# Waits in the order of their producers, implied waits left out, one semaphore per queue for a channel tile's shift transfers

## The chip, the cores and the metric

The kernel runs on the 8 cores of one Trainium2 chip, the same program on each with its own data, and the cores exchange nothing. The time is that of the slowest core in device microseconds, the median of 3 runs. Engines are named as in the profile: PE (TensorE matmul), PEld (its weight load), DVE (VectorE), ACT (ScalarE), POOL (GpSimd), SP (SyncE). A q behind an engine's name is its sequencer, which waits and issues while the engine itself is idle.

## The reference

One inference step of an encoder trunk of four layers, D_MODEL 1024, D_INNER 2048, for 4 x 4096 prompt tokens and 8 x 32 sample tokens. Each layer is an RMSNorm with a shift and scale, an input projection, a mixer, a SiLU gate, an output projection and a residual add. The part that the change touches most is the mixer of layer 2:

```python
            a, ag, z = jnp.split(jnp.einsum('bsd,de->bse', h, w_in_c), 3, axis=-1)
            glu = a * jax.nn.sigmoid(ag)
            ext, conv_c_new = with_history(glu, hist_c, CCONV_W - 1)
            y = causal_depthwise_conv(ext, w_conv_c) + b_conv_c
            y = jax.nn.silu(layer_norm(y, ln_c_g, ln_c_b))
            out = jnp.einsum('bse,ed->bsd', y * jax.nn.silu(z), w_out_c)
```

The depthwise convolution has 31 taps, and each of the 2048 channels has its own taps.

## The kernel before

Each core takes 2048 prompt tokens (with a halo) and the 32 tokens of one sample. They are worked in two column groups: g = 0 (1074 columns) and g = 1 (1056 columns, the sample's 32 among them). The program goes layer 0 to 3, in each layer g = 0 and then g = 1, and for each an input phase (`in_phase0` to `in_phase3`) and an output phase (`out_phase`). Channels lie on the 128 partitions, so D_INNER is 16 channel tiles, `c` = 0 to 15. Weights come through a ring of 8 tiles of 512 KB (`ring`, slots `rs.0` to `rs.7`), whose loads POOL issues as slots are released. PSUM is used as two slots of three banks, in turn (`next_slot`).

All instructions are recorded in program order by the class `Sched`, which makes one stream for each engine. An operation names the keys that it reads and writes (`t.N` are 64-word blocks of the scratch tile `tmp`, `bk.N` PSUM banks). `_deps` looks up who last wrote and read those keys, and gives a list of (semaphore, value) to wait for. Each entry becomes a wait instruction of its own ahead of the operation (L109 for operations, L129 for DMAs). In the kernel before, the list has the order in which keys were looked up, reads first, and a wait is left out only if this engine has itself waited for that semaphore at that value or above. Each DMA `slot` has a semaphore of its own, which counts 16 for each DMA.

The layer 2 input phase, `in_phase2`, is a pipeline over channel tiles. In step `i` stand, in program order:

- `front(i)`: two input projections on PE (`sg` and `sa`, 24 matmuls each, L461). ACT makes the sigmoid (L885), and DVE multiplies the two into the bf16 tile `G[i % 2]` (L893). For g = 0 two small DVE operations follow (L897, L899). For g = 1 DVE first copies the history into `G` (L890, L891), and two small ones end it (L902, L904).
- `square(i-4)` on ACT (L958), `conv(i-2)` on PE (64 matmuls of 32 output rows, L937) and its eviction on ACT into `Y` (L945), `stats(i-4)` on PE (L966).
- `spread(i)`: 16 DMAs of some 68 KB copy `G` into the shifted layout `R[i % 2]` in SBUF, 8 from SP and 8 from POOL, and DVE builds the tap weights (L920). `conv(i)` reads `R` two steps later.
- `gather(i-2)`: 2 DMAs on SP bring `Y` back into `ysT`.

The first matmul of the next `front` needs the PSUM slot that DVE's L893 (g = 1: L904) has to read first. After the last step the pipeline drains: `conv(14)`, `conv(15)`, their gathers, squares and statistics, with the z projections (`zmm`, L461, evicted by ACT at L978) in between; then the means are broadcast (L1000) and the tiles are normalised.

The transfers of `spread` before, for i of 16, SP where i is even and POOL where it is odd:

```python
                s.dma(("sp", "pool")[r], "gr%d_%d" % (ci, i), R[64 * r:64 * r + 64, j, 0:RW], bass.AP(g.tensor, g.offset, [list(g.ap[0]), [1, 4], [1, RW]]),
                      reads=tk(GB[ci], 560), writes=["R%d.%d" % (ci, i)] + (tk(RB[ci], 2240) if i < 2 and c < 2 else []))
```

The keys `tk(RB[ci], 2240)` of the scratch area under `R` are written only in the first two steps of a group, by the first SP transfer and the first POOL transfer, since that area was last used for something else.

## Time and profile before

| | before |
|---|---|
| time, median of 3 runs (lowest to highest) | 2282.03 us (2281.91 to 2287.24) |
| profiled execution, span of its slowest core (5) | 2280.8 us |
| spans of the 8 cores | 2267.7 to 2280.8 us |
| PE busy | 2135.5 us, 94% of the span |
| DVE, ACT, POOL busy | 46%, 29%, 14% |
| granted TensorE clock, mean of core 5 | 0.978 |
| layer 2 input phase, conv steps of g = 0 and g = 1 | about 1243 to 1395 us and 1553 to 1700 us |

The page gives the profiled execution by its span, which ends with the last instruction on the core; it has no other time of that execution. The median of the runs lies 1.2 us above this span, which is what lies around it. PE is the busy engine, so what counts is what PE waits for; the rest of the time that other engines lose is hidden.

### The profile page before, as it was taken

How to read it: one execution, taken by the hardware profiler on the slowest of the kernel's cores; microseconds unless marked ns; L12 is line 12 of the kernel's file. 1: busy time of each engine (PE TensorE's matmuls, PEld its weight loads, DVE VectorE, ACT ScalarE, POOL GpSimd, SP SyncE). 2: the span in 40 equal slices, each digit the busy share in tenths (PEclk: the TensorE clock that was granted, in tenths of full speed). 3: DMA queues.
4: the chain of work that ended last, by engine and by line, in shares of the span. 5: the costliest groups of instructions: out<-in, count | busy, mean ns of one | idle time of the engine just before them, and what ended most of it. 6: DMA issues, size and time to landing. Idle time of an engine off the chain costs nothing.

```text
span 2280.8 us, 41000 instructions; the slowest of 8 cores (2267.7 to 2280.8 us)
## 1 busy us (share of the span) xinstructions
PE 2135.5 (94%) x15851; PEld 1324.3 (58%) x15851; DVE 1045.9 (46%) x1482; ACT 670.2 (29%) x854; POOL 321.1 (14%) x593
## 2 busy tenths in 40 slices
PE   4999999998999999999999997999989999999996
PEld 1644655445666666666666664566655566666653
DVE  3444150442455454655545322753316566455535
ACT  3254303543011112111121334703446322303331
POOL 1012001111000100001002441104430000000000
PEclk9999999999999999999999998999999999999998
DMA  9905848057344644346445994538974444444423
GB/s 204 203 24 89 134 74 134 16 91 141 65 67 69 105 69 81 65 75 111 75 75 112 192 195 97 104 64 192 200 173 70 81 68 73 73 71 69 81 45 150
DMA packets 90637, 232.43 MB, mean 102 GB/s; under 512 B 16400, under 2 KB 41616, under 8 KB 90288
## 3 DMA queue, kind: packets, MB, share of 16 engines
q0 software_dynamic: 53264, 181.82, 45.3%
q1 hardware_dynamic: 37184, 48.00, 7.9%
q8 instruction: 130, 2.13, 0.4%
q14 instruction: 59, 0.48, 0.1%
HBM read 339.51 MB, written 9.55 MB: 153 GB/s over the span
## 4 chain that ended last, share of the span: by engine, by line
PE 82%; DVE 6%; DMA 5%; issue 2%; ACT 2%; SPq 2%; DVEq 0%; POOL 0%; ACTq 0%; POOLq 0%
PE ps L461 73%; PE ps L684 5%; DMA ring<-w_in_a 2%; SPq L130 2%; DMA ring<-w_ada 1%; PE ps L937 1%; DMA tmp<-tmp 1%; DVE tmp L893 1%; PE ps L753 1%; PE ps L749 1%; ACT hT L400 1%; DVE xb_sb L536 1%; DVE tmp L1007 1%; DMA xa_sb<-xa 0%; DVE xa_sb L536 0%
## 5 line engine op out<-in xcount | busy, mean ns | idle before, releaser
L461 PE MATMUL ps<-hT,ring 128*128 128x352 bf16 (+1 forms) x8448 | 1304.6, 316 | 30.3 <-DVE tmp L893 6.3
L461 PEld LDWEIGHTS ps<-hT,ring 128*128 128x128 bf16 x8448 | 827.8, 98 | 501.2 <-issue 50.5
L461 PE MATMUL ps<-ysT,ring 128*128 128x352 bf16 (+1 forms) x3072 | 473.6, 315 | 16.7 <-DVE xb_sb L542 4.8
L461 PEld LDWEIGHTS ps<-ysT,ring 128*128 128x128 bf16 x3072 | 298.7, 98 | 191.6 <-issue 26.2
L130 POOL DMA_DIRECT2D tmp<-tmp x256 | 128.7, 509 | 125.2 <-DVE histG L899 46.2
L684 PE MATMUL ps<-ring,hT 128*128 128x512 bf16 (+1 forms) x576 | 128.8, 383 | 4.2 <-DMA ring<-w_in_a 2.9
L893 DVE TENSOR_TENSOR tmp<-tmp,ps 128x1074 bf16<-128x1074 f32 (+3 forms) x64 | 45.5, 711 | 172.5 <-issue 97.5
L810 ACT ACTIVATE tmp<-ps 128x1074 f32<-128x1074 f32 (+1 forms) x32 | 33.9, 1058 | 261.9 <-PE ps L461 188.0
L820 DVE TENSOR_TENSOR tmp<-tmp,ps 128x1074 f32<-128x1074 f32 (+3 forms) x64 | 45.4, 710 | 140.0 <-PE ps L461 136.3
L945 ACT ACTIVATE tmp<-ps,cst_sb 128x16 bf16<-128x16 f32 (+2 forms) x160 | 69.8, 436 | 121.7 <-PE ps L937 103.4
L536 DVE SCALAR_TENSOR_TENSOR xb_sb<-ps,modT,xb_sb 128x1056 f32<-128x1056 f32 x32 | 42.1, 1317 | 128.5 <-PE ps L461 128.5
L536 DVE SCALAR_TENSOR_TENSOR xa_sb<-ps,modT,xa_sb 128x1074 f32<-128x1074 f32 (+1 forms) x32 | 42.1, 1325 | 122.8 <-PE ps L461 122.8
L684 PEld LDWEIGHTS ps<-ring,hT 128*128 128x128 bf16 (+1 forms) x576 | 55.9, 98 | 70.6 <-issue 7.6
L130 POOL DMA_DIRECT2D ring<-w_in_b x64 | 34.4, 538 | 386.0 <-PE ps L461 378.8
L837 DVE SCALAR_TENSOR_TENSOR tmp<-tmp,cst_sb 128x1074 f32<-128x1074 f32 (+1 forms) x64 | 85.1, 1329 | 7.0 <-DVE tmp L834 0.5
L841 ACT ACTIVATE ysT<-ps 128x1074 bf16<-128x1074 f32 (+1 forms) x32 | 33.9, 1058 | 184.2 <-PE ps L461 184.2
L1126 ACT ACTIVATE tmp<-ps 128x1056 f32<-128x1056 f32 (+3 forms) x64 | 39.1, 611 | 157.4 <-PE ps L461 154.5
L937 PE MATMUL ps<-tmp 128*32 128x352 bf16 (+2 forms) x2048 | 68.1, 287 | 10.5 <-DMA tmp<-tmp 8.3
L771 DVE TENSOR_TENSOR ysT<-ysT,tmp 128x1074 bf16<-128x1074 bf16 (+1 forms) x32 | 22.8, 713 | 108.0 <-ACT tmp L770 108.0
L844 DVE TENSOR_TENSOR tmp<-tmp,ps 128x1074 f32<-128x1074 f32 (+3 forms) x64 | 45.4, 709 | 55.0 <-PE ps L461 51.3
L760 DVE TENSOR_TENSOR ysT<-ps,ysT 128x512 bf16<-128x512 f32 (+2 forms) x72 | 44.1, 649 | 48.1 <-PE ps L753 47.5
L937 PEld LDWEIGHTS ps<-tmp 128*32 128x32 bf16 x2048 | 48.0, 99 | 30.7 <-issue 20.4
(156 smaller groups left out, 1667.2 us busy)
## 6 DMA issues: line engine op xcount, KB each, us to landing
ring<-w_in_b POOLq DMA_DIRECT2D x64, 512.0 KB, 5.3
ring<-w_ada POOLq DMA_DIRECT2D x48, 512.0 KB, 9.2
ring<-w_in_a POOLq DMA_DIRECT2D x48, 512.0 KB, 13.1
ring<-w_in_c POOLq DMA_DIRECT2D x48, 512.0 KB, 6.0
ring<-w_in_d POOLq DMA_DIRECT2D x32, 512.0 KB, 5.2
tmp<-tmp SPq DMA_DIRECT2D x128, 69.4 KB, 7.4
tmp<-tmp POOLq DMA_DIRECT2D x128, 69.4 KB, 6.8
tmp<-tmp SPq DMA_DIRECT2D x128, 67.5 KB, 5.7
```

Source lines behind the costliest of these rows:

```text
L130: h.dma_start(out=out, in_=in_, **kw).then_inc(dsm, 16)
L461: ins = h.matmul(PSB[:, 3 * sl + n, 0:W], lhsT=lw, rhs=rh[:, n * W:(n + 1) * W], start=(first and k == 0), stop=(last and k == len(pairs) ...
L536: s.op("dve", lambda h, sl=sl, xv=xv, d=d: h.scalar_tensor_tensor(out=xv, in0=PSB[:, 3 * sl:3 * sl + 3, 0:W], scalar=gate[:, 16 + d, 0:1], ...
L684: ins = h.matmul(PSB[0:n, nq, :], lhsT=hT[:, kh * 4 + kk, hc:hc + n], rhs=vw[nq * 2 + kh][:, kk, :], start=(kh == 0 and kk == 0), stop=(kh ...
L760: s.op("dve", lambda h, bank=bank, y=y: h.tensor_tensor(out=y, in0=v3(PSB[:, 4 + bank, :], 4)[:, :, 0:no], in1=y, op=ALU.mult), reads=yk, ...
L820: s.op("dve", lambda h, ps=ps, cc=cc, n=n, nb=nb, smp=smp, p=p, CG=CG: h.tensor_tensor(out=shp(p[:, H + cc + smp * H:H + cc + smp * H + n] ...
L837: s.op("dve", lambda h, p=p, a=a, c=c, wd=wd, k=k: h.scalar_tensor_tensor(out=a[:, 0:wd], in0=p[:, k:k + wd], scalar=prmT[:, c, k:k + 1], ...
L844: s.op("dve", lambda h, ps=ps, cc=cc, n=n, nb=nb, smp=smp, a=a, CG=CG: h.tensor_tensor(out=shp(tf(CG + cc, n), nb), in0=shp(a[:, cc + smp ...
L893: s.op("dve", lambda h, ps=ps, cc=cc, n=n, nb=nb, smp=smp: h.tensor_tensor(out=even_odd(G, H + cc + smp * H, n, nb), in0=pairs(tf(SIG + cc ...
L937: ins = h.matmul(PSB[32 * j:32 * j + 32, 3 * sl + bank, at:at + n], lhsT=wd[:, 4 * hf + j, b, :], rhs=R[:, 4 * hf + j, 4 * b + m0:4 * b + ...
L945: s.op("act", lambda h, hf=hf, bank=bank, at=at, o=o, k=k, d=d: h.activation(out=Y[:, hf, d:d + k], in_=PSB[:, 3 * sl + bank, at + o:at + ...
L1126: s.op("act", lambda h, ps=ps, cc=cc, n=n, nb=nb, smp=smp, pv=pv: h.activation(out=shp(pv[:, H + cc + smp * H:H + cc + smp * H + n], nb), ...
```

## The change

`_deps` sorts the waits by the place at which their producer was recorded, and goes through them from the latest to the earliest. Each kept wait also marks everything as seen that its producer had itself seen (`past`), so that an earlier wait which the later one implies is left out. What is left is emitted earliest producer first. A DMA's producer state is that of the queue that issued it. `dma_group` issues several DMAs behind one list of waits, all counting on one semaphore. `spread` now makes two groups, 8 transfers on SP (`gr<ci>_0`) and 8 on POOL (`gr<ci>_1`), and `gather` one group of 2 (`gy<ci>`). In the first two steps both groups of `spread` write the keys of the scratch area.

```diff
--- before.py
+++ after.py
@@ -51,6 +51,8 @@
         self.seen = {e: {} for e in ENGS}
         self.res = {}
         self.sem = {}
+        self.at = {}
+        self.past = {}
         for e in ENGS:
             self.sem[e] = nc.alloc_semaphore("p_" + e)
             self.cnt[e] = 0
@@ -77,15 +79,23 @@
                 for sname, v in r[1].items():
                     if sname != eng or k[:2] == "t.":
                         add((sname, v))
+        seen = self.seen[eng]
+        todo = sorted(((a, v) for a, v in waits.items() if seen.get(a, 0) < v), key=lambda e: self.at[e])
         out = []
-        for sname, v in waits.items():
-            if self.seen[eng].get(sname, 0) >= v:
+        for n in range(len(todo) - 1, -1, -1):
+            a, v = todo[n]
+            if seen.get(a, 0) >= v:
                 continue
-            self.seen[eng][sname] = v
-            out.append((sname, v))
+            out.insert(0, todo[n])
+            for b, w in self.past[todo[n]].items():
+                if w > seen.get(b, 0):
+                    seen[b] = w
+            seen[a] = max(v, seen.get(a, 0))
         return out
 
-    def _mark(self, src, val, reads, writes):
+    def _mark(self, src, val, reads, writes, eng=None):
+        self.at[(src, val)] = len(self.at)
+        self.past[(src, val)] = dict(self.seen[eng or src])
         for k in writes:
             self.res[k] = [(src, val), {}]
         for k in reads:
@@ -130,7 +140,27 @@
             h.dma_start(out=out, in_=in_, **kw).then_inc(dsm, 16)
 
         self.streams[q].append(emit)
-        self._mark(slot, val, reads, writes)
+        self._mark(slot, val, reads, writes, q)
+
+    def dma_group(self, q, slot, moves, reads=(), writes=()):
+
+        if slot not in self.sem:
+            self.sem[slot] = self.nc.alloc_semaphore("d_" + slot)
+            self.cnt[slot] = 0
+        waits = self._deps(q, reads, writes)
+        self.cnt[slot] += 16 * len(moves)
+        val = self.cnt[slot]
+        wl = [(self.sem[a], v) for a, v in waits]
+        dsm = self.sem[slot]
+
+        def emit(h):
+            for sm, v in wl:
+                h.wait_ge(sm, v)
+            for out, in_ in moves:
+                h.dma_start(out=out, in_=in_).then_inc(dsm, 16)
+
+        self.streams[q].append(emit)
+        self._mark(slot, val, reads, writes, q)
 
     def wait_all(self, eng, keys):
         waits = self._deps(eng, keys, keys)
@@ -908,11 +938,13 @@
             ci = c % 2
             R = v3(tb(RB[ci], 4480), 8)
             G = tb(GB[ci], GW)
-            for i in range(16):
-                j, r = i // 2, i % 2
-                g = G[16 * j:16 * j + 16, r * GH + CO // 2:r * GH + CO // 2 + RW]
-                s.dma(("sp", "pool")[r], "gr%d_%d" % (ci, i), R[64 * r:64 * r + 64, j, 0:RW], bass.AP(g.tensor, g.offset, [list(g.ap[0]), [1, 4], [1, RW]]),
-                      reads=tk(GB[ci], 560), writes=["R%d.%d" % (ci, i)] + (tk(RB[ci], 2240) if i < 2 and c < 2 else []))
+            for r in range(2):
+                moves = []
+                for j in range(8):
+                    g = G[16 * j:16 * j + 16, r * GH + CO // 2:r * GH + CO // 2 + RW]
+                    moves.append((R[64 * r:64 * r + 64, j, 0:RW], bass.AP(g.tensor, g.offset, [list(g.ap[0]), [1, 4], [1, RW]])))
+                s.dma_group(("sp", "pool")[r], "gr%d_%d" % (ci, r), moves, reads=tk(GB[ci], 560),
+                            writes=["R%d.%d" % (ci, r)] + (tk(RB[ci], 2240) if c < 2 else []))
             wd = tb(WD[ci], 1024).rearrange("p (a m r) -> p a m r", a=32, r=2)
             mk = bass.AP(dmask.tensor, dmask.offset, [list(dmask.ap[0]), [0, 32], [1, 16], [0, 2]])
             wt = wrepT[:, c, :]
@@ -937,7 +969,7 @@
                             ins = h.matmul(PSB[32 * j:32 * j + 32, 3 * sl + bank, at:at + n], lhsT=wd[:, 4 * hf + j, b, :],
                                            rhs=R[:, 4 * hf + j, 4 * b + m0:4 * b + m0 + n], start=(b == 0 and at == 0), stop=(b == 3), skip_group_check=True)
                 return ins
-            s.op("pe", f, reads=["R%d.%d" % (ci, i) for i in range(16)] + tk(RB[ci], 2240) + tk(WD[ci], 512), writes=sk(sl))
+            s.op("pe", f, reads=["R%d.%d" % (ci, r) for r in range(2)] + tk(RB[ci], 2240) + tk(WD[ci], 512), writes=sk(sl))
             Y = v3(tb(YB[ci], 2 * HC), 2)
             for hf, bank, at, n, m0 in parts:
                 segs = [(0, n, m0)] if g == 0 or m0 == 0 else [(0, NPA // 2 - m0, m0), (n - 16, 16, NPA // 2)]
@@ -950,13 +982,12 @@
 
             ci = c % 2
             Y = v3(tb(YB[ci], 2 * HC), 2)
-            for hf in range(2):
-                s.dma("sp", "gy%d_%d" % (ci, hf), v3(ysT[64 * hf:64 * hf + 64, c, 0:NC], 2), Y[:, hf, :],
-                      reads=tk(YB[ci], HC), writes=["ysh%d.%d" % (hf, c)] + (["ys.%d" % c] if hf == 0 else []))
+            s.dma_group("sp", "gy%d" % ci, [(v3(ysT[64 * hf:64 * hf + 64, c, 0:NC], 2), Y[:, hf, :]) for hf in range(2)],
+                        reads=tk(YB[ci], HC), writes=["ys.%d" % c])
 
         def square(c):
             s.op("act", lambda h: h.activation(out=tb(SQ, NC), in_=ysT[:, c, 0:NC], func=AF.Square),
-                 reads=["ys.%d" % c, "ysh0.%d" % c, "ysh1.%d" % c], writes=tk(SQ, NC // 2))
+                 reads=["ys.%d" % c], writes=tk(SQ, NC // 2))
 
         def stats(c):
             def f(h):
@@ -966,7 +997,7 @@
                         ins = h.matmul(PSB[32 * q:32 * q + 32, b, 0:W], lhsT=onesE, rhs=src[:, q * W:(q + 1) * W],
                                        start=(c == 0), stop=(c == 15), skip_group_check=True)
                 return ins
-            s.op("pe", f, reads=["onesE", "ys.%d" % c, "ysh1.%d" % c] + tk(SQ, NC // 2), writes=bk(6, 7))
+            s.op("pe", f, reads=["onesE", "ys.%d" % c] + tk(SQ, NC // 2), writes=bk(6, 7))
 
         def zmm(c):
             spec = ("in2", 16 + c // 2, g)
@@ -1005,7 +1036,7 @@
 
         def center(c):
             s.op("dve", lambda h: h.tensor_tensor(out=tf(TT[c % 3], NC), in0=ysT[:, c, 0:NC], in1=tf(MEAN, NC), op=ALU.subtract),
-                 reads=["ys.%d" % c, "ysh1.%d" % c] + tk(MEAN, NC), writes=tk(TT[c % 3], NC))
+                 reads=["ys.%d" % c] + tk(MEAN, NC), writes=tk(TT[c % 3], NC))
 
         def norm(c):
             t = tf(TT[c % 3], NC)
```

Counted over the built programs, wait instructions go from 1692 to 1120 on PE, from 1853 to 1388 on DVE, from 1089 to 804 on ACT, from 905 to 326 on POOL and from 424 to 138 on SP. No other instruction is added, removed or moved on any engine.

On DVE, at steps 3 and 4 of the layer 2 input phase for g = 0, the multiplication into `G` (L893 before, L923 after) stands behind the waits in brackets (`d_` is a DMA slot's semaphore, `p_` an engine's). Before:

```order
712 L893 TENSOR_TENSOR tmp<-tmp,ps 128x3x2x179 [waits p_act,p_pe,d_gr1_0,d_gr1_1,d_gr1_2,d_gr1_3,d_gr1_4,d_gr1_5,d_gr1_6,d_gr1_7,d_gr1_8,d_gr1_9,d_gr1_10,d_gr1_11,d_gr1_12,d_gr1_13,d_gr1_14,d_gr1_15]
713 L897 TENSOR_SCALAR tmp<-tmp,cst_sb 128x2x15 [waits p_dve]
714 L899 COPY histG<-tmp 128x2x15 [waits p_dve]
715 L920 TENSOR_TENSOR tmp<-dmask,wrep_sb 128x1024 [waits p_pe]
716 L893 TENSOR_TENSOR tmp<-tmp,ps 128x3x2x179 [waits p_act,p_pe,d_gr0_0,d_gr0_1,d_gr0_2,d_gr0_3,d_gr0_4,d_gr0_5,d_gr0_6,d_gr0_7,d_gr0_8,d_gr0_9,d_gr0_10,d_gr0_11,d_gr0_12,d_gr0_13,d_gr0_14,d_gr0_15]
717 L897 TENSOR_SCALAR tmp<-tmp,cst_sb 128x2x15 [waits p_dve]
```

After:

```order
700 L923 TENSOR_TENSOR tmp<-tmp,ps 128x3x2x179 [waits d_gr1_1,p_act,p_pe]
701 L927 TENSOR_SCALAR tmp<-tmp,cst_sb 128x2x15 [waits p_dve]
702 L929 COPY histG<-tmp 128x2x15 [waits p_dve]
703 L952 TENSOR_TENSOR tmp<-dmask,wrep_sb 128x1024 [waits p_pe]
704 L923 TENSOR_TENSOR tmp<-tmp,ps 128x3x2x179 [waits d_gr0_0,d_gr0_1,p_act,p_pe]
705 L927 TENSOR_SCALAR tmp<-tmp,cst_sb 128x2x15 [waits p_dve]
```

The 16 waits on transfers that stood behind `p_pe` become two, and they stand ahead of it.

On POOL, at the start of the same phase, its half of `spread` for steps 0, 1 and 2 (`tmp<-tmp`) with the ring loads between. Before:

```order
201 L130 DMA tmp<-tmp 64x1x540 [waits p_dve,d_gr0_0]
202 L130 DMA tmp<-tmp 64x1x540 x7
203 L130 DMA ring<-w_in_c 128x2048 [waits d_rs0,p_pe]
204 L130 DMA ring<-w_in_c 128x2048 [waits d_rs1]
205 L130 DMA tmp<-tmp 64x1x540 [waits p_dve,d_gr1_0]
206 L130 DMA tmp<-tmp 64x1x540 x7
207 L130 DMA tmp<-tmp 64x1x540 [waits p_dve,d_gr0_1,p_pe]
208 L130 DMA tmp<-tmp 64x1x540 [waits d_gr0_3]
209 L130 DMA tmp<-tmp 64x1x540 [waits d_gr0_5]
```

After:

```order
74 L160 DMA tmp<-tmp 64x1x540 [waits d_gr0_0]
75 L160 DMA tmp<-tmp 64x1x540 x7
76 L140 DMA ring<-w_in_c 128x2048 [waits p_pe]
77 L140 DMA ring<-w_in_c 128x2048
78 L160 DMA tmp<-tmp 64x1x540 [waits d_gr1_0]
79 L160 DMA tmp<-tmp 64x1x540 x7
80 L160 DMA tmp<-tmp 64x1x540 [waits p_dve,p_pe]
81 L160 DMA tmp<-tmp 64x1x540 x7
```

In steps 0 and 1 the wait on the semaphore of one SP transfer (`d_gr0_0`, before) is now a wait under the same name for the whole SP group, value 128 and not 16 in g = 0; from step 2 on a wait is left only ahead of the first transfer.

On ACT, at the drain of the phase for g = 0, the evictions of the second and third z projection (L978 before, L1009 after) and the last squares (L958, after L989). Before:

```order
313 L945 ACTIVATE tmp<-ps,cst_sb 128x352 [waits p_act]
314 L945 ACTIVATE tmp<-ps,cst_sb 128x176 [waits p_act]
315 L958 ACTIVATE tmp<-ysT 128x1056 [waits d_gy0_0,d_gy0_1,p_pe]
316 L978 ACTIVATE tmp<-ps 128x1056 [waits p_pe,d_gr0_0,d_gr0_1,d_gr0_2,d_gr0_3,d_gr0_4,d_gr0_5,d_gr0_6,d_gr0_7,d_gr0_8,d_gr0_9,d_gr0_10,d_gr0_11,d_gr0_12,d_gr0_13,d_gr0_14,d_gr0_15]
317 L978 ACTIVATE tmp<-ps 128x1056 [waits p_pe,p_dve,d_gr1_0,d_gr1_1,d_gr1_2,d_gr1_3,d_gr1_4,d_gr1_5,d_gr1_6,d_gr1_7,d_gr1_8,d_gr1_9,d_gr1_10,d_gr1_11,d_gr1_12,d_gr1_13,d_gr1_14,d_gr1_15]
318 L958 ACTIVATE tmp<-ysT 128x1056 [waits d_gy1_0,d_gy1_1,p_act]
```

After:

```order
305 L977 ACTIVATE tmp<-ps,cst_sb 128x176 [waits p_act]
306 L989 ACTIVATE tmp<-ysT 128x1056 [waits d_gy0,p_pe]
307 L1009 ACTIVATE tmp<-ps 128x1056 [waits p_pe] x2
308 L989 ACTIVATE tmp<-ysT 128x1056 [waits d_gy1]
309 L1009 ACTIVATE tmp<-ps 128x1056 [waits p_pe]
```

The two evictions lose the waits on `spread`'s transfers, 16 each.

## Rows read from the trace of the kernel before

**Rows 1.** page, part 1: busy us, share of the span, instructions

```profile
PE 2135.5 (94%) x15851; PEld 1324.3 (58%) x15851; DVE 1045.9 (46%) x1482; ACT 670.2 (29%) x854; POOL 321.1 (14%) x593
```

**Rows 2.** waits of PE, whole span: us in total, times, longest

```profile
PE ps L966 <- ACT tmp L958: 12.9, 5, 5.2
PE ps L937 <- DMA tmp<-tmp: 8.3, 3, 5.8
...
PE ps L461 <- DVE tmp L893: 6.3, 13, 0.8
```

**Rows 3.** chain that ended last, 1283.6 to 1287.2 us: start, us, what

```profile
1284.13 0.02 DVEq L109
...
1285.23 0.02 DVEq L109
...
1285.30 1.28 DVE tmp L893
...
1286.72 0.62 PE ps L461 x3
```

**Rows 4.** waits of PE in the stretch 1250 to 1366 us

```profile
PE ps L461 <- DVE tmp L893: 4.8, 11, 0.7
```

**Rows 5.** timeline of PE, 1243 to 1247 us: start, us, what, idle before

```profile
1243.43 1.99 PE L937 MATMUL ps<-tmp 128*32 128x352 bf16 x64
1246.13 1.08 PE L461 MATMUL ps<-hT,ring 128*128 128x358 bf16 x6 [0.70 <-DVE tmp L893]
```

**Rows 6.** timeline of POOL, 1230 to 1245 us

```profile
1233.84 4.06 POOL L130 DMA_DIRECT2D tmp<-tmp  x8 [12.06 <-DMA tmp<-tmp]
1237.80 1.22 POOL L130 DMA_DIRECT2D ring<-w_in_c  x2
1244.30 1.05 POOL L130 DMA_DIRECT2D tmp<-tmp  x2 [5.28 <-DMA tmp<-tmp]
```

**Rows 7.** spread's SP transfers, 1230 to 1236 us: duration ns min/median/max, first and last start

```profile
L130 SPq DMA_DIRECT2D tmp<-tmp x8: 571/579/697, 1230.7 to 1235.1; - x8
...
DMA to landing us min/median/max: 2.4/2.5/4.0
```

**Rows 8.** spread's SP transfers, 1237.9 to 1243 us, by tile

```profile
DMA to landing us min/median/max: 5.6/6.8/8.0
```

**Rows 9.** timeline of POOL, 1538 to 1566 us

```profile
1543.97 4.25 POOL L130 DMA_DIRECT2D tmp<-tmp  x8 [12.18 <-DMA tmp<-tmp]
1548.30 1.11 POOL L130 DMA_DIRECT2D ring<-w_in_c  x2
1551.97 4.24 POOL L130 DMA_DIRECT2D tmp<-tmp  x8 [2.56 <-DMA tmp<-tmp]
```

**Rows 10.** spread's SP transfers, 1540 to 1547 us, by tile

```profile
L130 SPq DMA_DIRECT2D tmp<-tmp x8: 544/545/1506, 1540.9 to 1546.4; - x8
...
DMA to landing us min/median/max: 2.4/2.9/3.7
```

**Rows 11.** timeline of PE, 1552 to 1567 us

```profile
1555.31 7.32 PE L461 MATMUL ps<-hT,ring 128*128 128x352 bf16 x48 [0.32 <-DVE outS L904]
1563.96 2.04 PE L937 MATMUL ps<-tmp 128*32 128x352 bf16 x64 [1.33 <-DMA tmp<-tmp]
```

**Rows 12.** timeline of DVE, 1551 to 1556 us

```profile
1551.30 0.18 DVE L890 COPY tmp<-histG 128x30 bf16<-128x30 bf16 x1 [2.17 <-DMA tmp<-tmp]
...
1553.19 1.78 DVE L893 TENSOR_TENSOR tmp<-tmp,ps 128x704 bf16<-128x704 f32 x3 [1.42 <-PE ps L461]
```

**Rows 13.** chain that ended last, 1377 to 1425 us

```profile
1382.74 0.05 issue
...
1385.99 5.42 DMA tmp<-tmp
...
1403.64 0.04 issue
...
1404.62 0.04 ACT tmp L978
```

## The prediction

> **What bounds the kernel now.** PE is busy for 2135.5 us of a span of 2280.8 [rows 1], so only what PE waits for counts, some 145 us. I first read PE's own list of waits, to see whom it waits for. Most of it is start-up, norm statistics and phase ends, which this change leaves. Three rows belong to the layer 2 input phase, where nearly all the removed waits stand [rows 2]: PE waits for DVE's L893 13 times for 6.3 us, for `spread`'s transfers 3 times for 8.3 us, and for the squares of ACT (L958) 5 times for 12.9 us.
>
> Next I read the chain of waits inside one step, 1283.6 to 1287.2 us [rows 3]. PE ends `sa` and DVE takes its semaphore at 1284.13. Then DVE stands through 16 further waits, one each 0.069 us ((1285.23 - 1284.13) / 16), all long satisfied, since they are for transfers of two steps ago. L893 runs only from 1285.30, 1.17 us after its last real input. It ends after 1.28, and PE starts the next `front` at 1286.72, some 0.4 us late. The reader is to see that DVE is idle and still late.
>
> Third, the timelines of PE, POOL and SP at the start of the phase, since the order on POOL shows a new wait there. Conv step 0 runs at 1243.43 with no idle time ahead of it [rows 5], though PE passes 17 waits before it: PE's sequencer does them while earlier matmuls run.
>
> **Part 1: waits on PE.** 572 fewer. I cost them at nothing: their cover is the queue of matmuls in front (rows 5). Where PE has run dry and waits for a transfer, a few tenths a time come back; that happens 3 times [rows 2], and is inside part 4.
>
> **Part 2: 16 waits behind `p_pe` on DVE, g = 0.** They become two and stand ahead of `p_pe`. L893 starts 16 x 0.069 = 1.1 us earlier. PE's wait per step is 0.4 to 0.8, so it goes whole. Total 6.3 us in 13 stalls [rows 2]; the first two, 0.70 each ([rows 5], and the longest of [rows 4]), lie where part 3 acts and are counted there. Left: 6.3 - 1.4 = 4.9 us. The rest of the 1.1 has no taker: next PE is limited by its own matmuls. Bounds 4.0 (some steps late for another reason) and 5.8 (the restart after a wait costs a little more than the idle time shown). In g = 1 the 16 waits stand ahead of L890, before `sa` is done, so nothing is won there.
>
> One rule of the Trainium skill speaks against this part: in "VectorE: DVE Perf Modes", section "The DRAIN you can't avoid", a semaphore after each DVE operation costs nothing extra, as the pipeline's drain covers it. By that reading the term would be 0 and the sum 4.9 us higher. The trace differs here, at 0.069 us a wait with the engine idle (rows 3), and the trace decides.
>
> **Part 3: POOL now waits for the whole SP group, steps 0 and 1.** Both groups write the keys of the scratch area, so POOL's first transfer, which waited for SP's first one, waits for all eight. The rows show this wait already as idle time ended by a DMA [rows 6, 9]. Queued behind it on POOL: its 8 transfers, two ring loads, the next step's 8. Waiting for these: `conv(0)`, `conv(1)`, and DVE's L893 or L890 two steps on. The ring loads have spare time, since eight tiles stand in the ring and a pair lasts two steps.
>
> g = 0, step 0: SP's eighth issue is at 1235.1 and a landing takes 2.4 to 4.0 [rows 7], so POOL starts at 1237.5 to 1239.1 and not 1233.84 [rows 6]. Its eighth issue comes 3.5 later (4.06 for eight, rows 6) and lands 2.4 to 4.0 later: 1243.4 to 1246.6, I take 1244.3. `conv(0)` stood at 1243.43, so it is 0.9 late; but the next `front` waited 0.70 for L893, which is gone, and comes at about 1246.4 against 1246.13: +0.3. Step 1: SP's group landed in 5.6 to 8.0 [rows 8], behind the ring loads of 1237.80 [rows 6]. These now leave after POOL's group, near 1241.5. So the SP landings fall nearer 2.5, the last at 1245 to 1250, and POOL's second group goes out from there and not from 1244.30; it now stands behind the ring loads. It lands at 1251 to 1260, I take 1255; `conv(1)` would be due at 1254 and is 1 late, less the second 0.70 stall: about +0.7 over both steps, bounds -1 and +6.
>
> g = 1, step 0: the eighth SP issue is at 1546.4, and would be near 1545.3 without the one of 1.5 us; landing 2.4 to 3.7 [rows 10]. POOL starts at 1547.7 to 1550.1 and not 1543.97 [rows 9]; its last transfer lands at 1554 to 1558, I take 1555.7. DVE's L890 waits for it, 1551.30 before [rows 12], and from L890 to the next `front` lie 4.0 us, of which DVE idles 1.42 for PE (rows 12) that is by then done: 2.6 us, with the small waits 2.8. So the next `front` comes at 1558.5 and not 1555.31: +3.2. Step 1: `conv(1)` stood at 1563.96 after 1.33 idle on a transfer [rows 11]. Now it is due at 1558.5 + 7.3 = 1565.8, and POOL's second group should be in by then, since the ring loads of 1548.30 (rows 9) have moved behind the SP group. With the 0.3 of the following stall gone: +1.5 over both steps, bounds 0 and +4.5.
>
> Part 3 in sum: +2.2 us, bounds -1 and +10. The Trainium skill, "DMA: Bandwidth & Descriptors", section "Queues, rings and completion order", has it that each DMA engine takes turns between queues but keeps the order inside one, so POOL's group has to follow its own ring loads while SP's need not. By that rule the second groups tend to the late ends, 2 to 3 us above my value.
>
> **Part 4: the drain.** (a) ACT passes its waits between the end of the z matmuls, 1403.64, and L978 at 1404.62 [rows 13]: 17 of 0.055 us, of which 16 go, 0.9 us. The last square, its statistics and PE follow at once. The same pair stands in g = 1: -1.8, bounds -1.6 and -1.9. (b) `conv(15)` of g = 0 hangs on `spread(15)`, whose chain is L893, eight SP issues with 0.05 for a wait between (rows 13), and a landing of 5.42. L893 starts 1.1 earlier and the SP waits give 0.4: -1.5, bounds 0 (the transfers are late anyway, the landing being twice that of rows 7) and -4 (the gather before it gets ahead of the ring load). (c) In g = 1 only the 0.4 and a few tenths of PE's waits: -0.5, bounds 0 and -2. Sum -3.8.
>
> **Part 5: all other dropped waits** (ACT, POOL, SP): each gives some 0.06 us only where PE waits for that very operation, a handful of phase ends: -0.3.
>
> **The sum** against the profiled span of 2280.8: +2.2 - 4.9 - 3.8 - 0.3 = -6.8, so 2274.0. The median of the runs lies 1.2 above the span, so 2275.2, rounded to 2275.
>
> **The rivals.** (R1) The gain is eaten: steps of g = 0 become 0.4 shorter but the transfers don't, and PE finds `spread` or the squares late instead. For it: PE already waits for transfers and for ACT in this phase (rows 2). Against: the transfers that the 16 waits of rows 3 ask for are two steps old and have all landed, so 0.4 a step doesn't use up their slack. Then part 2 and the drain give 2 and 2 us, part 3 costs 2.2: 2280. (R2) Slower: POOL's late start decides. For it: the landings under ring loads, 8.0 (rows 8), and PE's 1.33 at 1563.96. Price: part 3 at its upper bound, +10, against -4.0 - 1.6 - 0.3: 2286. It turns the sign when part 3 costs over 9 us, that is when `conv(0)` and `conv(1)` are each over 2 us late in both groups. It would pass the bound for slower only if `conv(2)` were late too. (R3) The drain collapses: the gather whose landing stalls the squares gets ahead of the ring load, and of the 12.9 us (rows 2) 5 more go: 2269.
>
> **Chances.** Forecast, 2270 to 2279: 0.60. R1, 2279 to 2283: 0.20. R2, 2283 and above: 0.12. R3, below 2270: 0.08. A measurement of this kernel can tell about 0.3%, 6.8 us, so the lines are 2275.2 and 2288.9. My forecast lies on the first, which splits its case: 0.37 of it faster, and all of R3; slower only a third of R2 and little else. That gives faster 0.45, same 0.50, slower 0.05. The range leaves out half of R3 and some of R2: 2267 to 2285.
>
> **What would show it.** Right: no wait of PE for DVE's multiplication (L923 after) from step 3 on in g = 0, steps 0.4 us shorter; DVE's `p_pe` wait followed at once by the multiplication; POOL's first `spread` transfer of each group 4 to 6 us later and ended by a DMA; an idle PE before `conv(0)` in both groups; no gap of 0.9 before ACT's third z eviction. Wrong: `conv(1)` and `conv(2)` late by more than 2 us in either group (R2), steps as long as before (R1), or a drain that differs by more than 4 us either way.

## The result, and the profile after

The changed kernel takes 2290.12 us (median of 11 runs, 2287.7 to 2310.65), the kernel before, run beside it, 2284.92 (median of the 9 runs compared, 2281.91 to 2288.11). The ratio is 1.0042, 95% interval 1.0025 to 1.0060: 9.6 us slower, where I had forecast 2275 and a range that ended at 2285. In three of the eleven runs (2306.05, 2307.67 and 2310.65 us), as in some runs of e2 to e6 and e8 below and in one of the kernel before beside them, two cores had a granted clock of 0.96 to 0.97, for a reason that stays open; they are in the ratios, and without them the means lie 4.1 us apart, ratio 1.0018. So the change makes the kernel slower, by 4 to 10 us; the traces below say 5.6.

The profiles are of the slowest core, core 5 before and core 4 after. The page's first part, which answers to [rows 1], shows PE 5.5 us busier with the same number of instructions:

```profile
PE 2141.0 (94%) x15851; PEld 1327.9 (58%) x15851; DVE 1047.2 (46%) x1482; ACT 671.1 (29%) x854; POOL 311.2 (14%) x593
```

PE's waits over the whole span (us in total, times, longest) answer to [rows 2]. The line numbers have moved: L966 is now L997, L937 is L969, L461 is L491, L893 is L923.

```profile
PE ps L969 <- DMA tmp<-tmp: 28.9, 7, 6.5
...
PE ps L997 <- ACT tmp L989: 5.4, 4, 2.3
```

PE's wait for DVE's multiplication, 6.3 us before, is no longer in the list, and its wait for ACT's squares has fallen from 12.9 to 5.4. But its wait for `spread`'s transfers has risen from 8.3 to 28.9. Of this, 16.1 us lie in steps 0 and 1 of the two groups (1.3 before), and 12.8 in the drains (7.0 before), where it only takes the place of the wait for the squares. PE's timelines at `conv(15)` of g = 0, before and after:

```profile
1389.81 0.48 PE L966 MATMUL ps<-ysT,onesE 128*32 128x352 bf16 x3 [5.16 <-ACT tmp L958]
...
1391.76 3.71 PE L937 MATMUL ps<-tmp 128*32 128x352 bf16 x64 [1.18 <-DMA tmp<-tmp]
```

```profile
1387.32 0.33 PE L997 MATMUL ps<-ysT,onesE 128*32 128x352 bf16 x3 [0.55 <-ACT tmp L989]
...
1394.32 3.71 PE L969 MATMUL ps<-tmp 128*32 128x352 bf16 x64 [6.52 <-DMA tmp<-tmp]
```

Two gains and one larger loss: each has its place.

**The gain in a step.** DVE's and PE's timelines in a middle step of g = 0:

```profile
1291.44 1.27 DVE L923 TENSOR_TENSOR tmp<-tmp,ps 128x1074 bf16<-128x1074 f32 x1 [6.52 <-PE ps L491]
```

```profile
1291.26 1.99 PE L969 MATMUL ps<-tmp 128*32 128x352 bf16 x64
1293.08 0.32 PE L997 MATMUL ps<-ysT,onesE 128*32 128x352 bf16 x3
1293.23 0.32 PE L997 MATMUL ps<-tmp,onesE 128*32 128x352 bf16 x3
1293.48 7.53 PE L491 MATMUL ps<-hT,ring 128*128 128x358 bf16 x48
1300.94 1.99 PE L969 MATMUL ps<-tmp 128*32 128x352 bf16 x64
```

DVE's idle time is now ended by PE, no longer by 1.1 us of its own waits [rows 3]; L491 has no idle time before it, and from conv to conv lie 1300.94 - 1291.26 = 9.68 us, where 10.15 lay before.

**The loss.** POOL's timeline at the start of g = 0, which answers to [rows 6]:

```profile
1237.82 4.07 POOL L160 DMA_DIRECT2D tmp<-tmp  x8 [16.40 <-DMA tmp<-tmp]
1241.79 1.22 POOL L140 DMA_DIRECT2D ring<-w_in_c  x2
1251.86 8.11 POOL L160 DMA_DIRECT2D tmp<-tmp  x16 [8.84 <-DMA tmp<-tmp]
```

SP's eight transfers of step 1, by tile (ns min/median/max, first and last start; then issue to landing):

```profile
L160 SPq DMA_DIRECT2D tmp<-tmp x8: 545/608/1437, 1237.6 to 1243.1; - x8
...
DMA to landing us min/median/max: 3.2/4.3/8.1
```

The two ring loads are issued at 1241.79 and after, while SP issues the last of its eight. A landing takes up to 8.1 us, and it is the last transfer's, so SP's group is complete at about 1243.1 + 8.1 = 1251.2. Only then may POOL begin its second group, at 1251.86. PE's timeline shows what that costs:

```profile
1244.49 1.99 PE L969 MATMUL ps<-tmp 128*32 128x352 bf16 x64 [1.35 <-DMA tmp<-tmp]
1246.41 7.53 PE L491 MATMUL ps<-hT,ring 128*128 128x358 bf16 x48
1260.08 3.71 PE L969 MATMUL ps<-tmp 128*32 128x352 bf16 x64 [6.14 <-DMA tmp<-tmp]
1263.73 8.24 PE L491 MATMUL ps<-hT,ring 128*128 128x358 bf16 x48
```

`conv(1)` stands still for 6.14 us, and then its 64 matmuls take 3.71 us instead of 1.99, and the next `front` 8.24 instead of 7.53. On the eight cores this stall is 5.5 to 6.6 us (before: 0 to 1.7), and `conv(1)` takes 3.71 on each. The stretches of the same place give the reason (us, PE busy, granted clock, DMA share, GB/s):

```profile
1246.00:1254.00 8.00, 7.94 (x68) 1.00 0.91 192
1254.00:1260.00 6.00, 0.00 (x0) 0.87 0.82 183
1260.00:1264.00 4.00, 3.92 (x66) 0.50 0.84 155
1264.00:1271.00 7.00, 7.00 (x43) 0.91 0.97 225
```

After the idle stretch the granted clock is 0.50, the lower level, 1.2 GHz. That adds 3.71 - 1.99 + 8.24 - 7.53 = 2.4 us on this core to a stall of 6.1. The second group repeats it: POOL's and PE's timelines there answer to [rows 9, 11]:

```profile
1550.85 4.07 POOL L160 DMA_DIRECT2D tmp<-tmp  x8 [16.42 <-DMA tmp<-tmp]
1554.82 1.21 POOL L140 DMA_DIRECT2D ring<-w_in_c  x2
1566.57 8.11 POOL L160 DMA_DIRECT2D tmp<-tmp  x16 [10.54 <-DMA tmp<-tmp]
```

```profile
1575.23 3.82 PE L969 MATMUL ps<-tmp 128*32 128x352 bf16 x64 [6.48 <-DMA tmp<-tmp]
```

**Where the time went.** For a ledger I took from PE's timeline of each core the start of `conv(0)`, `conv(3)`, `conv(13)` and of the first broadcast matmul of the means (L1000 before, L1031 after), in both groups. The column "to g1" runs from the last broadcast of the norm statistics (L423 before, L453 after) to `conv(0)` of g = 1. Each value is the median over the six cores whose matmul records are complete. The last column but one is the sum of the seven; the last is the mean measured time less that of the kernel before beside it, without the runs named above. The short names are those of the experiments below.

| us | g0 conv 0-3 | g0 3-13 | g0 13-bcast | to g1 conv 0 | g1 conv 0-3 | g1 3-13 | g1 13-bcast | sum | time less before |
|---|---|---|---|---|---|---|---|---|---|
| before | 30.4 | 101.8 | 37.6 | 59.7 | 30.7 | 97.4 | 37.2 | 394.8 | |
| after | 36.9 | 96.8 | 34.9 | 62.3 | 37.5 | 96.1 | 35.9 | 400.4 | +4.1 |
| no wait for SP (e1) | 28.5 | 96.8 | 35.9 | 62.1 | 30.1 | 96.1 | 34.5 | 384.0 | -13.9 |
| that wait alone (e2) | 36.5 | 101.8 | 37.2 | 63.8 | 31.3 | 97.3 | 37.1 | 405.0 | +12.9 |
| it in step 0 only (e15) | 32.0 | 96.8 | 35.3 | 62.3 | 31.7 | 96.4 | 35.3 | 389.8 | -5.9 |
| ring loads held (e5) | 30.7 | 100.6 | 35.8 | 62.1 | 33.3 | 97.6 | 35.2 | 395.3 | -0.8 |
| only groups (e4) | 35.6 | 96.8 | 34.8 | 63.5 | 33.7 | 96.5 | 35.6 | 396.5 | +5.6 |
| waits sorted and dropped (e14) | 29.2 | 96.8 | 34.4 | 59.7 | 29.4 | 96.9 | 35.6 | 382.0 | -13.9 |
| sorted only (e8) | 29.4 | 96.8 | 35.1 | 59.7 | 30.2 | 97.2 | 35.4 | 383.8 | -12.6 |
| dropped only (e13) | 30.3 | 101.5 | 36.1 | 59.7 | 29.8 | 97.1 | 35.2 | 389.7 | -8.1 |
| step 0 single (e10) | 30.3 | 96.8 | 34.5 | 59.7 | 32.6 | 96.1 | 34.1 | 384.1 | -13.9 |
| single, no wait (e11) | 28.5 | 96.8 | 35.7 | 63.1 | 30.0 | 96.7 | 35.2 | 386.0 | -10.2 |

After against before, the two starts (conv 0-3) cost 6.5 + 6.8 = 13.3 us and the way to `conv(0)` of g = 1 2.6; the middles give back 5.0 + 1.3 and the drains 2.7 + 1.3. That is +5.6, beside a measured +4.1; in the other kernels too the two agree within 4 us. The two profiled spans, 2280.8 and 2289.4, lie further apart (8.6), but they are one execution each. Left out is what lies between the columns, in the main the output phase: counted from the first matmul behind the broadcasts that end the drain, it takes 72 us on some cores and 74 on others, in the kernel before (five cores and three) as in the changed one (three and five); why is open.

### The profile page after: what moved, and what is told of

Its sections match the earlier page's. It is cut to its first block, busy times and chain, and to the rows that moved or that the text cites. A ratio compares the mean times of both kernels' runs of the same rounds, so it can differ in the third digit from the quotient of the medians.

```text
span 2289.4 us, 38813 instructions; the slowest of 8 cores (2269.6 to 2289.4 us)
## 1 busy us (share of the span) xinstructions
PE 2141.0 (94%) x15851; PEld 1327.9 (58%) x15851; DVE 1047.2 (46%) x1482; ACT 671.1 (29%) x854; POOL 311.2 (14%) x593
## 4 chain that ended last, share of the span: by engine, by line
PE 84%; DMA 5%; DVE 5%; ACT 2%; issue 2%; SPq 1%; POOL 1%; DVEq 0%; ACTq 0%; POOLq 0%
PE ps L491 73%; PE ps L714 5%; PE ps L969 3%; DMA tmp<-tmp 2%; DMA ring<-w_in_a 1%; DMA ring<-w_ada 1%; SPq L160 1%; PE ps L783 1%; PE ps L779 1%; ACT hT L430 1%; DVE xb_sb L566 1%; DVE tmp L1038 1%; DMA xa_sb<-xa 0%; DVE xa_sb L566 0%; PE ps L997 0%
## 5 line engine op out<-in xcount | busy, mean ns | idle before, releaser
L491 PE MATMUL ps<-hT,ring 128*128 128x352 bf16 (+1 forms) x8448 | 1305.1, 316 | 21.1 <-DVE ysT L790 5.1
L491 PEld LDWEIGHTS ps<-hT,ring 128*128 128x128 bf16 x8448 | 828.1, 99 | 491.8 <-issue 41.0
L491 PE MATMUL ps<-ysT,ring 128*128 128x352 bf16 (+1 forms) x3072 | 474.1, 315 | 16.4 <-DVE xb_sb L572 4.8
L491 PEld LDWEIGHTS ps<-ysT,ring 128*128 128x128 bf16 x3072 | 298.9, 98 | 191.5 <-issue 25.8
L923 DVE TENSOR_TENSOR tmp<-tmp,ps 128x1074 bf16<-128x1074 f32 (+3 forms) x64 | 45.5, 711 | 174.6 <-PE ps L491 153.2
L969 PE MATMUL ps<-tmp 128*32 128x352 bf16 (+2 forms) x2048 | 72.5, 299 | 29.0 <-DMA tmp<-tmp 28.9
L140 POOL DMA_DIRECT2D ring<-w_in_b x64 | 34.5, 540 | 385.9 <-PE ps L491 378.7
L969 PEld LDWEIGHTS ps<-tmp 128*32 128x32 bf16 x2048 | 50.8, 103 | 50.1 <-issue 38.7
## 6 DMA issues: line engine op xcount, KB each, us to landing
tmp<-tmp SPq DMA_DIRECT2D x128, 67.5 KB, 4.0
```

Source lines behind the costliest of these rows:

```text
L491: ins = h.matmul(PSB[:, 3 * sl + n, 0:W], lhsT=lw, rhs=rh[:, n * W:(n + 1) * W], start=(first and k == 0), stop=(last and k == len(pairs) ...
L923: s.op("dve", lambda h, ps=ps, cc=cc, n=n, nb=nb, smp=smp: h.tensor_tensor(out=even_odd(G, H + cc + smp * H, n, nb), in0=pairs(tf(SIG + cc ...
L969: ins = h.matmul(PSB[32 * j:32 * j + 32, 3 * sl + bank, at:at + n], lhsT=wd[:, 4 * hf + j, b, :], rhs=R[:, 4 * hf + j, 4 * b + m0:4 * b + ...
```

## The experiments

The rival theories for the loss: **T1**, POOL's wait for SP's whole group; **T2**, eight transfers back to back on one semaphore crowd each other whoever waits; **T3**, the size of T1 comes from the ring loads that now fall among SP's last transfers; and the clock, which adds to a stall. For the gain: the order of the waits, or their number. Times are medians of the runs compared, ratios are to the kernel before on the same chip.

### The wait taken away, and put alone

e1, in the changed kernel, both groups of `spread` wait only for the earlier users of the scratch area:

```diff
+            area = {k: s.res.get(k) for k in tk(RB[ci], 2240)} if c < 2 else None
...
-                            writes=["R%d.%d" % (ci, r)] + (tk(RB[ci], 2240) if c < 2 else []))
+                            writes=["R%d.%d" % (ci, r)] + (tk(RB[ci], 2240) if c < 2 and r == 0 else []), area=area if r else None)
```

> The changed kernel, but in steps 0 and 1 of each group the POOL group waits only for the earlier users of the scratch area, no longer for the SP group. T1 (the cross wait is what costs): the stalls of 6.14 and 6.48 us before conv(1) go, and with them the 1.8 us each that conv(1)'s own matmuls then ran slower at half clock; 2 x (6.3 + 1.8) and about 1 us less at each conv(0) make some 15 us off the changed kernel's 2290, so about 2275 to 2277, ratio to before 0.995 to 0.997. T2 (eight transfers issued back to back on one semaphore crowd each other, whoever waits): conv(1) stays 4 us or more late, and the time is above 2283.

2272.19 us, ratio 0.9930 (0.9901 to 0.9958). POOL's timeline of this kernel, start of g = 0:

```profile
1227.98 4.06 POOL L165 DMA_DIRECT2D tmp<-tmp  x8 [9.38 <-DVE histG L934]
1233.55 1.11 POOL L140 DMA_DIRECT2D ring<-w_in_c  x2 [1.51 <-PE ps L496]
1235.31 4.06 POOL L165 DMA_DIRECT2D tmp<-tmp  x8 [0.64 <-DVE histG L934]
```

POOL's second group follows the first by 7.3 us and not by 14.0, its idle time is ended by DVE, and the three convs of g = 0 are 9.4 us apart. On no core does `conv(1)` wait any more, in either group. T1 holds, and the eight back to back are no burden there. In g = 1, though, `conv(0)` still waits 1.7 to 3.3 us for transfers (before: 0 on all cores); the last experiments come back to it. The time came out some 3 us better than expected.

e2, the reverse, in the kernel before:

```diff
-            for i in range(16):
+            for i in list(range(0, 16, 2)) + list(range(1, 16, 2)):
...
-                      reads=tk(GB[ci], 560), writes=["R%d.%d" % (ci, i)] + (tk(RB[ci], 2240) if i < 2 and c < 2 else []))
+                      reads=tk(GB[ci], 560) + (["R%d.%d" % (ci, k) for k in range(0, 16, 2)] if i == 1 and c < 2 else []), writes=["R%d.%d" % (ci, i)] + (tk(RB[ci], 2240) if i < 2 and c < 2 else []))
```

> The kernel before, its waits as they were and one semaphore for each transfer, with SP's eight transfers recorded first and, in steps 0 and 1, POOL's first transfer waiting for all eight of SP's. T1: conv(1) becomes 5 to 6.5 us late in each group and runs at half clock, and nothing is given back: 12 to 17 us over before, ratio 1.005 to 1.0075. T2: POOL's wait alone does little, within 3 us of before.

2299.01 us, ratio 1.0056 (1.0029 to 1.0083), some 13 us. PE's timeline of core 4 of this kernel:

```profile
1259.94 3.71 PE L937 MATMUL ps<-tmp 128*32 128x352 bf16 x64 [5.37 <-DMA tmp<-tmp]
```

The same stall and slow conv, with sixteen single semaphores, though from core to core it varies more here, 1.0 to 6.6 us. In g = 1 the loss shows before `conv(0)` (+4.1) more than in the convs (+0.6). T2 is out as the main cause.

### One part of the change at a time

e3 and e14 are one kernel: before, with the new `_deps` and `_mark` and nothing of `dma_group`. Of its diff, the line in `dma`:

```diff
-        self._mark(slot, val, reads, writes)
+        self._mark(slot, val, reads, writes, q)
```

> The kernel before with only the new order of the waits and the dropping of implied ones; one semaphore for each transfer stays. T1: steps 3 to 12 of the first group 9.7 us each as in the changed kernel (before: 10.15), the drain up to 4 us shorter, conv(1) not late by more than 1 us: 7 to 12 us faster than before, 2274 to 2279, ratio 0.995 to 0.997. T2 (the gain comes from fewer semaphores, not from the order of the waits): steps stay at 10.1 us, within 3 us of before.

2271.28 us, ratio 0.9934 (0.9904 to 0.9964); steps of 9.68, and `conv(1)` of g = 0 waits 0.3 to 2.7 us, not 5.5 to 6.6. The gain is larger than I expected of it, see e13.

e4 is the complement, the groups with the old `_deps`:

```diff
-        todo = sorted(((a, v) for a, v in waits.items() if seen.get(a, 0) < v), key=lambda e: self.at[e])
...
+        for sname, v in waits.items():
+            if self.seen[eng].get(sname, 0) >= v:
```

> The changed kernel with the waits in the old order and none dropped: only the grouped transfers with one semaphore for each queue. T1: conv(1) as late as in the changed kernel (6 us in each group, half clock after it). If DVE's eviction of a step still asks for its buffer first and for the matmul last, the steps of the first group stay at 9.7 to 9.8 us, since only two waits are left where sixteen were, and the time is within 3 us of the changed kernel, 2288 to 2293, ratio 1.001 to 1.005. Rival: with the old order the steps go back to 10.1 us, and the time is 4 to 5 us over the changed kernel, about 2295.

2292.63 us, ratio 1.0045 (1.0007 to 1.0082): like the whole change within the intervals, and in the expected band. Its `conv(1)` of g = 0 waits 5.92 us and takes 3.61, and its steps 3 to 12 are at 9.68. So the groups alone bring the loss, and each of the two halves of the change alone brings the gain in a step.

e9 has the edits of e1 and of e4 together, the old `_deps`, groups, and no wait of POOL for SP:

> The kernel before with its grouped transfers on one semaphore a queue, the old order of waits, nothing dropped, and no wait of POOL's group for SP's. If the groups bring by themselves what the order of the waits brings (two waits in DVE's eviction in place of sixteen), it lies at 2272 to 2277, as the two kernels with the new order and no late group. If the groups bring nothing, it lies at 2283 to 2288.

2278.23 us, ratio 0.9963 (0.9949 to 0.9977), a little over the expected band: groups do bring it, when nothing is late.

### Order or number

e8 sorts the waits of before and drops none; e13 drops the implied ones and leaves the old order. Their `_deps`, e8 first:

```diff
+        todo = sorted(((a, v) for a, v in waits.items() if seen.get(a, 0) < v), key=lambda e: self.at[e])
+        seen.update(todo)
+        return todo
```

```diff
+            took.add(todo[n])
...
+        return [e for e in waits.items() if e in took]
```

> The kernel before with its waits sorted by their producers, and none dropped as implied: the same waits as before, in another order. If the place of DVE's sixteen waits, behind the wait for the matmul, was the cost, the steps 3 to 12 of the first group are 9.68 us as with both edits, and the time is that of both, 2270 to 2275. If their number was the cost (PE's 572 among them), the steps stay at 10.1 us and the time is within 3 us of before, 2285.

> The kernel before with the implied waits dropped but the rest left in the old order (572 fewer on PE alone). My prediction gave the dropped waits no worth of their own: steps 3 to 12 of the first group stay at 10.1 us and the time within 3 us of before. Rival: in DVE's eviction most of the sixteen waits are implied by a later one and go too; then the steps fall to 9.7 us without any sorting, and the time is 2272 to 2277.

Sorting only: 2275.08 us, 0.9967 (0.9937 to 0.9996), or 12.6 us by the ledger's last column. Dropping only: 2280.76 us, 0.9965 (0.9951 to 0.9979), 8.1 us. DVE's multiplication in a middle step of g = 0, dropped only:

```profile
1296.16 1.27 DVE L903 TENSOR_TENSOR tmp<-tmp,ps 128x1074 bf16<-128x1074 f32 x1 [7.09 <-issue]
```

and sorted only:

```profile
1290.01 1.27 DVE L894 TENSOR_TENSOR tmp<-tmp,ps 128x1074 bf16<-128x1074 f32 x1 [6.52 <-PE ps L462]
```

With the dropped waits alone DVE still idles 7.09 us up to an "issue", its sixteen transfer waits behind `p_pe`; sorted, with the same sixteen ahead of it, the idle time is 0.57 shorter and PE ends it. So in the steps the order is everything (101.5 against 96.8 us for ten), as I had said. But my expectation for e13, no gain, failed: its drains are 1.5 and 2.0 us shorter, and the ratio says some 8 us in all. The columns of its row add up to 5.1 us less than those of before; the rest I can't place.

> The kernel before with the new order and dropped waits, a second time, beside the three others of this call, so that they are compared on one chip: 2270 to 2275. It also tells whether dropping adds to ordering, whose own ratio was 0.9967 against 0.9934 for both, with intervals that overlap.

2274.40 us, 0.9935 (0.9919 to 0.9951). Dropping and sorting overlap and do not add up: by the ledger's sums dropping alone gives 5.1 us, sorting alone 11.0, both 12.8, so that beside sorted waits dropping is worth some 2 us. (The three ratios seem to add, 0.0035 + 0.0033 = 0.0068 against 0.0065, but sorting's 12.6 us in the ledger's last column are 0.0055.)

### The price of step 0, of step 1 and of the ring loads

e6 and e15 are one kernel: e1 with the wait kept in step 0 and taken away in step 1:

```diff
-                            writes=["R%d.%d" % (ci, r)] + (tk(RB[ci], 2240) if c < 2 and r == 0 else []), area=area if r else None)
+                            writes=["R%d.%d" % (ci, r)] + (tk(RB[ci], 2240) if c == 0 or (c == 1 and r == 0) else []), area=area if r and c == 1 else None)
```

> The changed kernel with the wait of POOL's group for SP's group kept in step 0 and taken away in step 1. If the cost is made in step 1 alone (POOL's second group waits for SP's second, and that is late), conv(1) is on time within 1 us and the time is that of the kernel without both waits, 2272 to 2276. If step 0's wait does it too, by pushing POOL's second group and the ring loads behind, conv(1) stays 2 to 4 us late and the time is 2279 to 2284.

> The kernel with POOL's wait for SP's group kept in step 0 and taken away in step 1, a second time. Its first measurement has three runs at 2276.0 to 2280.8 us and three at 2295.1 to 2297.3, and the profiled one has two cores at a granted clock of 0.968 from before the first step on. If step 1 alone makes the loss, undisturbed runs lie at 2276 to 2281 again, some 10 us under the changed kernel; what remains over the kernel without both waits, 2272.5, is step 0's wait, 4 to 8 us. If the upper three are its true time, the wait in step 0 costs as much as both.

First 2287.97 us, 1.0000 (0.9966 to 1.0035), in the two clusters named there; then 2278.55 us, 0.9974 (0.9962 to 0.9986). I go by the second, whose interval is narrow. POOL's and PE's timelines of e15:

```profile
1234.28 4.06 POOL L165 DMA_DIRECT2D tmp<-tmp  x8 [16.43 <-DMA tmp<-tmp]
1238.24 1.22 POOL L140 DMA_DIRECT2D ring<-w_in_c  x2
1239.33 4.20 POOL L165 DMA_DIRECT2D tmp<-tmp  x8
```

```profile
1242.13 3.37 PE L975 MATMUL ps<-tmp 128*32 128x352 bf16 x64 [2.56 <-DMA tmp<-tmp]
```

POOL starts as late as in the changed kernel (16.43 idle), `conv(0)` is 2.56 late, but the second group goes out 5.1 us after the first. The ledger splits the loss in three, from the kernel with sorted and dropped waits alone (e14, sum 382.0) to the changed one (400.4). Groups without any wait for SP (e1, 384.0) cost 2.0 us, which is about the 2.4 more before `conv(0)` of g = 1. Step 0's wait (e15, 389.8) adds 5.8, of which 3.5 + 1.6 in conv 0-3. Step 1's wait adds 10.6, nearly all of it the 4.9 + 5.8 of conv 0-3. The measured times, each against the kernel before on its own chip, say 0, 8.0 and 10.0. So step 1 makes the larger part, and step 0 is not small. The late `conv(0)` of g = 1 is not the wait's alone: 62.3 us in the changed kernel and in e15, and 62.1 in e1, which has no such wait.

e5, the changed kernel with the two loads of step 1 released at the end of step 3:

```diff
-            if i % 2 == 1:
-                for sp in specs:
+            if i == 1:
+                held = list(specs)
+                hook(0)
+            elif i % 2 == 1:
+                for sp in held + specs:
```

> The changed kernel, with the two weight slots of step 1 released, and so the two ring loads that refill them issued, only at the end of step 3 instead of step 1. T3 (the ring loads issued in the middle of SP's third group take the place of its last transfers, and so make POOL's second group late): POOL's second group starts by about 1248 in place of 1251.86, conv(1) stalls 2 to 3 us in place of 6, and each group gains some 4 to 5 us: about 2281 to 2283, if the later loads make no stall of their own. Rival: POOL's second group waits for a group of eight transfers whatever runs beside it; conv(1) stalls over 5 us, and the time stays at 2288 to 2292.

2286.56 us, ratio 1.0014 (0.9971 to 1.0058). POOL and PE:

```profile
1235.56 4.06 POOL L160 DMA_DIRECT2D tmp<-tmp  x8 [16.42 <-DMA tmp<-tmp]
1244.26 8.05 POOL L160 DMA_DIRECT2D tmp<-tmp  x16 [4.64 <-DMA tmp<-tmp]
```

```profile
1253.64 1.99 PE L969 MATMUL ps<-tmp 128*32 128x352 bf16 x64 [1.33 <-DMA tmp<-tmp]
```

SP's landings of step 1 take 4.3 us at most in this kernel (changed kernel: 8.1):

```profile
L160 SPq DMA_DIRECT2D tmp<-tmp x7: 544/731/1082, 1235.3 to 1240.1; - x7
...
DMA to landing us min/median/max: 2.9/3.4/4.3
```

POOL's first wait is the same, but the second group starts 8.7 us after the first (changed kernel: 14.0) and `conv(1)` is 1.33 late (6.14); over the eight cores 0 to 1.9 where it was 5.5 to 6.6: T3 holds. The loads held back then go out four at a time and give part of it back, 100.6 against 96.8 us in steps 3 to 13, as the last clause of the expectation allowed; so the time is not the 2281 to 2283 expected. (What the expectation calls SP's third group is its second, that of step 1.)

### The clock

e16, the changed kernel with this ahead of `conv(1)`:

```diff
+                for k in range(160):
+                    ins = h.matmul(PSB[32 * (k % 4):32 * (k % 4) + 32, 3 * sl, 0:n1], lhsT=wd[:, k % 4, 0, :], rhs=tb(WD[ci], 1024)[:, 0:n1],
```

> The changed kernel with 160 additional small matmuls ahead of conv(1) in each group, on operands that are there and into the buffer that conv(1) overwrites, so that TensorE works through most of the 6 us in which it waited; no wait is taken away. If the stall's idleness is what lowers the granted clock, conv(1) takes 2.0 us in place of 3.7 and 3.8, the next step 9.4 to 9.7 in place of 11.5 and 11.2, and the time is 3 to 4 us under the changed kernel, 2286 to 2287. If the clock falls for another cause, conv(1) stays at 3.7 and the time at 2290 or more.

Only two runs could be compared, 2288.78 and 2289.33 us, with no interval; they miss the 2286 to 2287 expected, and the time says little. The trace settles the point of the clock. PE's timeline:

```profile
1249.07 6.15 PE L975 MATMUL ps<-tmp 128*32 128x352 bf16 x160
1255.05 1.98 PE L969 MATMUL ps<-tmp 128*32 128x352 bf16 x64
1256.96 7.53 PE L491 MATMUL ps<-hT,ring 128*128 128x358 bf16 x48
```

With PE at work through the stall, conv takes 1.98 and not 3.71 us (1.98 to 1.99 on all eight cores), and the `front` behind it 7.53 and not 8.24. The stall's idleness is what lowers the clock. By the medians over eight cores conv 0-3 takes 34.4 and 35.9 us, against 36.9 and 37.2 in the changed kernel. So 2.5 + 1.3 = 3.8 us of the loss in both groups together are the clock's.

### Two attempts at a faster one

e10 is e1 with step 0's sixteen transfers single again, POOL's first behind SP's first; e11 is e3 without even that wait:

```diff
+            for i in range(16 if c == 0 else 0):
...
+            for r in range(2 if c else 0):
```

```diff
-                      reads=tk(GB[ci], 560), writes=["R%d.%d" % (ci, i)] + (tk(RB[ci], 2240) if i < 2 and c < 2 else []))
+                      reads=tk(GB[ci], 560), writes=["R%d.%d" % (ci, i)] + (tk(RB[ci], 2240) if i < 1 and c < 2 else []), area=area if i == 1 else None)
```

> The kernel without both waits of POOL for SP (new order of waits, groups), but step 0's sixteen transfers issued singly as before, POOL's first behind SP's first. If the late conv(0) of the second group (136.1 us from the end of the first group to it, against 132.7 with staggered single transfers) comes of both queues starting at once, this gives back some 3 us there: 2268 to 2271, the fastest so far. If not, 2272 as without it.

> The kernel before with the new order and dropped waits, single transfers, and POOL's first transfer of steps 0 and 1 no longer behind SP's first. POOL starts some 3 us sooner there. If that is worth anything, conv(1) loses its last 0.5 us of lateness in each group and the time is 2270 to 2272; if the crowding of both queues costs as much, it equals the kernel with the new order alone within 2 us, with a later conv(0).

e10: 2274.65 us, 0.9937 (0.9922 to 0.9952). The way to `conv(0)` of g = 1 is as short as with single transfers, 59.7, but the statistics ahead of `conv(3)` of g = 0 then wait 2.1 us for ACT's squares, and conv 0-3 takes 1.8 and 2.5 us more than in e1: the gain is given back. e11: 2277.59 us, 0.9951 (0.9933 to 0.9969), with 63.1 there. PE's timeline:

```profile
1547.24 3.55 PE L953 MATMUL ps<-tmp 128*32 128x352 bf16 x64 [3.00 <-DMA tmp<-tmp]
```

When both queues start at once, `conv(0)` of g = 1 is late (62.1 in e1, 63.1 here); staggered by one transfer it is not (59.7 in e14, and in every kernel of the ledger whose POOL waits for SP's first transfer alone). That much of T2 is true, and worth 2.4 to 3.4 us. Nothing beats e1, e3/e14 and e10, which lie together at 0.993 to 0.994; the simplest of them leaves `dma_group` out.

## Why the prediction was wrong

In one line: the waits gave 12.8 us by the ledger's sums, 13.9 by the times (e14; parts 1, 2, 4 and 5 said 9.0), and part 3 cost 18.4 or 18.0 (after against e14), not 2.2.

**Part 1, waits on PE at nothing**: not tested alone. e13 shows that all dropped waits together are worth 5 to 8 us in the kernel before, which parts 1, 4a and 5 put at 2.1. Undersized; 3.5 of it lies in the drains, the rest I can't give to an engine.

**Part 2, 4.9 us for DVE's waits**: right in place and size: steps 3 to 12 of g = 0 gave 5.0 us, none of it without the new order or fewer semaphores. (g = 1, where I had nothing, gave 1.3, of which e14 has 0.5.) The Trainium skill, "VectorE: DVE Perf Modes", section "The DRAIN you can't avoid", has it that a semaphore after each DVE operation costs nothing extra, from which I read 0 us. That is said of eight copies in a row and not of waits that an idle engine passes, and so gave no 0 for this term: e8, the same waits in another order, gained 5.0 us in these steps.

**Part 3, step 0**: the times were right, the price too low. POOL started at 1237.82 (said: 1237.5 to 1239.1), `conv(0)` waited 1.35 us (said: 0.9 late), and `conv(0)` of g = 1 came 2.6 us later (said: 3.2). But e14, e1 and e15 put the groups and step 0's wait together at 7.8 us, where I had 0.3 + 3.2: the steps behind are late as well. And the 2.6 is right partly by luck, since without the wait it is 2.4 (e1), for both queues then start at once.

**Part 3, step 1: the step that failed.** Of the 2.2 us of part 3, step 0 has 0.3 + 3.2, so that step 1 was put at -1.3; it cost 10.6 (e15 against the changed kernel). I wrote of the ring loads "These now leave after POOL's group, near 1241.5. So the SP landings fall nearer 2.5, the last at 1245 to 1250", and of g = 1 "POOL's second group should be in by then". The loads did leave at 1241.79. But SP's second group runs from 1237.6 to 1243.1, so that they fell among its last transfers, and the last landed near 1251.2, after 8.1 us and not 2.5. I had moved the loads to a new time and not asked what else runs at it. Before, POOL waited for SP's first transfer only, and such a late last one cost nothing; the new wait is for the last. So POOL's second group went out at 1251.86, `conv(1)` could start only at 1260.08, the late end of my 1251 to 1260, and waited 6.1 us where I had it 1 late. g = 1 did the same at 6.5, over its bound of 4.5 for both steps. To it comes the clock, which the sum left out: about 2 us a group (e16: 3.8 in both). The Trainium skill, "DMA: Bandwidth & Descriptors", section "Queues, rings and completion order": I had used its order inside one queue, by which POOL's group comes late behind its own ring loads. But the late landings were SP's, in another queue (8.1 us with the ring loads about, 4.3 without them in e5). For that the same section has another sentence, that a semaphore's increment lands only after every earlier write of that DMA engine, across its queues. The trace agrees with it (the last SP transfer lands at 1251.25, the second ring load at 1251.29); no run here separates it from mere sharing of the engines.

**Part 4, the drain, -3.8**: the sum is right, 2.7 + 1.3 = 4.0, its terms only in part. (a) ACT's and PE's timelines in g = 0 give the last z matmuls and the eviction behind them:

```profile
1402.57 3.75 PE L491 MATMUL ps<-hT,ring 128*128 128x352 bf16 x24
```

```profile
1406.42 1.05 ACT L1009 ACTIVATE tmp<-ps 128x1056 bf16<-128x1056 f32 x1 [3.04 <-PE ps L491]
```

ACT starts 0.10 us after PE's end, 0.98 before [rows 13]: right. (b) was not: from `conv(13)` to `conv(15)` of g = 0 it takes 15.9 us and took 16.2 (medians of the six cores), so 0.3 and not 1.5, since `conv(15)` now waits for `spread` what the statistics had waited for the squares. The rest of the 2.7 lies behind `conv(15)`, where beside ACT's 0.9 the next 24 matmuls of a z projection took 6.19 us at a granted clock of 0.59 in the profile before and 5.06 at 0.72 after (3.75 the ones ahead of them). No term of the prediction has that: the sum came out right by luck.

**Rivals.** R1 and R3 didn't happen (R3's 5 us under 2275.2 would be 2270, not the 2269 written). R2 named the mechanism, and its point of decision, over 9 us; I gave it 0.12 and bounded it at 10, because I let each conv be late by 2 us, with the landing under a ring load, 8.0 [rows 8], in hand. A sum that took that row for step 1 has SP's group in at 1243 + 8 = 1251, POOL's 3.5 + 2.4 to 4.0 later, and `conv(1)` 3 to 4.5 late against its 1254, in both groups: past the point of decision without any clock.

## What to carry to other kernels

Merging transfers under one semaphore turns every wait on the first into a wait on the last: look for ordering waits between the parts (here a scratch area's key written by both groups) and price them by the slowest landing, not the median. When a step moves, ask what runs at its new time. Where an engine stands idle and then late, put its old waits ahead of the one that is truly last; that alone was worth 0.5 us a step.

## What the runs showed of the hardware

A wait that has long been satisfied costs DVE 0.069 us when it stands behind the last one [rows 3], and nothing seen when ahead of it (e8). A 67.5 KB transfer of SP landed after 2.4 to 2.5 us with POOL's queue idle (step 0), after up to 4.3 beside POOL's eight (e5), and after up to 8.1 with two ring loads of 512 KB beside them as well (step 1 of the changed kernel). Six idle microseconds of TensorE were followed by 64 matmuls at half clock, and 160 small matmuls in the gap prevented it (e16). The length of a stall alone doesn't decide it: 2.56 us were followed by a conv of 3.37 us (e15), but 3.07 us by one of 1.99, as PE's timeline of e2 at `conv(0)` has it:

```profile
1242.87 1.99 PE L937 MATMUL ps<-tmp 128*32 128x352 bf16 x64 [3.07 <-DMA tmp<-tmp]
```
